# Rate and gate columns of the last two layers: weights stationary in four column groups, summed by a small product

## What is computed

```python
proj = h @ w_in                      # (256 tokens) x (1024) @ (1024) x (3592)
aq, ak, av, dn_qkv, dn_z, dn_b, dn_a = jnp.split(proj, cuts, axis=-1)
...
qkv = jax.nn.silu(causal_dwconv(dn_qkv, dn_conv_w)).astype(jnp.float32)
dq, dk, dv = jnp.split(qkv, [DELTA_K_WIDTH, 2 * DELTA_K_WIDTH], axis=-1)
beta = jax.nn.sigmoid(dn_b.astype(jnp.float32))
g = -jnp.exp(dn_a_log.astype(jnp.float32)) * jax.nn.softplus(
    dn_a.astype(jnp.float32) + dn_dt_bias.astype(jnp.float32))
```

## Time and profile before

| | |
|---|---|
| median of three runs | 1790.45 us (1787.21 to 1792.16) |
| profiled execution, span | 1787.4 us; the page gives no time around the span, so this stands for the execution's own time |
| TensorE busy (matmul) | 1560.1 us, 87% |
| VectorE, ScalarE, GpSimd busy | 53%, 30%, 33% |
| L926, both layers | 64 records, 8.1 us |
| L936, both layers | 48 records, 8.6 us |
| L942, both layers | 64 records, 27.9 us |

### The profile page before, as it was taken

One profiled execution on the slowest core, in us unless ns is written; L12 is line 12 of the kernel. 1 busy time (PEld: TensorE's weight loads), 2 busy tenths in 40 slices (PEclk: granted clock), 3 DMA queues, 4 the chain that ended last, 5 costly groups with the idle time before them and its releaser, 6 DMA issues.

```text
span 1787.4 us, 18463 instructions
## 1 busy us (share of the span) xinstructions
PE 1560.1 (87%) x5998; PEld 953.2 (53%) x5998; DVE 953.6 (53%) x2199; ACT 538.4 (30%) x1472; POOL 584.2 (33%) x595
## 2 busy tenths in 40 slices
PE   8998888986877676556469999999999999999997
PEld 2645463443444222222125867777774778677774
DVE  2586677767686868788873464212123335321222
ACT  2234334442433343323222363211111354211111
POOL 0000046777777777777750012100000002100000
PEclk9999999998989898777789999999999999999999
DMA  9965059999999999999996220844441421364410
GB/s 349 350 224 196 19 219 408 409 409 388 409 398 409 409 409 409 379 408 406 406 404 236 94 95 1 276 159 142 142 176 37 176 95 48 117 230 160 141 48 24
DMA packets 170581, 438.50 MB, mean 245 GB/s; under 512 B 12515, under 2 KB 58883, under 8 KB 170356
## 3 DMA queue, kind: packets, MB, share of 16 engines
q0 software_dynamic: 81824, 299.86, 43.0%
q1 hardware_dynamic: 88662, 137.46, 22.1%
HBM read 436.23 MB, written 1.05 MB: 245 GB/s over the span
## 4 chain that ended last, share of the span: by engine, by line
PE 56%; DMA 14%; DVE 10%; POOL 9%; issue 6%; DVEq 2%; ACT 2%; ACTq 0%; SPq 0%; POOLq 0%
PE psum L1150 15%; DMA arena<-in_expert_u,indices 14%; PE psum L1161 6%; POOL arena L1293 5%; PE psum L914 5%; POOL arena L1288 4%; DVE arena L2196 3%; PE psum L855 2%; PE psum L1175 2%; PE psum L452 2%; PE psum L1138 2%; PE psum L831 2%; PE psum L942 2%; PE psum L538 2%; PE psum L1104 1%
## 5 line engine op out<-in xcount | busy, mean ns | idle before, releaser
L817 PE MATMUL psum<-arena 128*128 128x512 f32 x382 | 240.8, 716 | 193.1 <-ACT arena L1561 189.9
L2196 DVE CUSTOM_DVE_ANT_0 arena<-arena,psum 128x1024 f32<-128x1024 f32 x224 | 273.6, 1221 | 125.6 <-DMA arena<-in_expert_u,indices 107.4
L1293 POOL DMA_INDIRECT arena<-in_expert_v,indices x256 | 255.5, 998 | 79.8 <-issue 70.7
L1288 POOL DMA_INDIRECT arena<-in_expert_u,indices x256 | 251.5, 983 | 89.5 <-issue 61.9
L1150 PE MATMUL psum<-activations_T,weight_ring 128*128 128x256 f32 x1280 | 279.2, 379 | 0.0
L1150 PEld LDWEIGHTS psum<-activations_T,weight_ring 128*128 128x128 f32 x1280 | 243.0, 190 | 39.8 <-issue 7.7
L817 PEld LDWEIGHTS psum<-arena 128*128 128x128 f32 x382 | 69.7, 213 | 335.5 <-ACT arena L1561 307.1
L2437 DVE SCALAR_TENSOR_TENSOR arena<-psum,small,arena 128x254 f32<-128x254 f32 (+1 forms) x176 | 76.8, 477 | 321.2 <-ACT arena L1714 317.9
L818 PE MATMUL psum<-arena 128*128 128x512 f32 x382 | 223.2, 670 | 0.0
L1243 POOL TENSOR_TENSOR small<-small 128x1 f32<-128x1 f32 (+4 forms) x29 | 30.4, 1049 | 539.7 <-DVE small L2309 199.2
L1549 ACT ACTIVATE activations_T<-activations_T 128x1 f32<-128x1 f32 x256 | 51.9, 203 | 396.8 <-DVE activations_T L2196 396.7
(11 more groups left out here) (402 smaller groups left out, 2056.1 us busy)
## 6 DMA issues: line engine op xcount, KB each, us to landing
weight_ring<-in_ffn_w_in SPq DMA_DIRECT2D x44, 1024.0 KB, 7.7
weight_ring<-in_w_in SPq DMA_DIRECT2D x14, 2048.0 KB, 10.3
arena<-in_ffn_w_out POOLq DMA_DIRECT2D x22, 1024.0 KB, 5.2
weight_ring<-in_w_ada SPq DMA_DIRECT2D x8, 2048.0 KB, 8.6
weight_ring<-in_w_out SPq DMA_DIRECT2D x6, 2048.0 KB, 7.8
weight_ring<-in_w_ada SPq DMA_DIRECT2D x16, 512.0 KB, 9.9
weight_ring<-in_w_pq SPq DMA_DIRECT2D x4, 2048.0 KB, 15.7
weight_ring<-in_w_in SPq DMA_DIRECT2D x2, 2080.0 KB, 8.0
```

The costliest lines, as they stand in the source:

```text
L817: mm(o0, DIAG[:, j % ND, :], VROWS[n % NV][:, 0:512], start=m == 0, stop=last)
L1288: nc.gpsimd.indirect_dma_start(UROWS[g % NU], None, a["expert_u"], bass.IndirectOffsetOnAxis(ap=where, axis=0)).then_inc(sem(f"u_row{g % N ...
L1293: nc.gpsimd.indirect_dma_start(VROWS[g % NV], None, a["expert_v"], bass.IndirectOffsetOnAxis(ap=where, axis=0)).then_inc(sem(f"v_row{g % N ...
L2196: ttr(out=DOTJ[n >= UNIT], in0=UROWS[n % NU], in1=h2, scale=1.0, scalar=0.0, op0=ALU.mult, op1=ALU.add, accum_out=DOT[:, i, m:m + 1]).then ...
```

## The change

The eight columns are computed the other way round: the weights are stationary and the 256 tokens move. 32 weight columns (488 to 519 of the slot, the last eight of them the wanted ones) are loaded into one of four column groups of the array, group k modulo 4 for the k-th block of 128 rows of the contraction. Each group adds up two of the eight blocks, on its own 32 partitions of one bank: eight products instead of sixteen. ScalarE copies the bank, 128 partitions by 256, to `BAC`. TensorE then takes two small products, one for each tile of 128 tokens, with `BAC` stationary and a 128x8 matrix `FOUR` moving. `FOUR` picks the wanted eight rows of each group, so the product adds the four groups and turns the result to tokens by eight columns. These small products stand between `wh` 0 and `wh` 1 of the transposes, and wait for the copy. ScalarE's two small copies move along with them. `FOUR` is made once, early, by three small additions on VectorE.

```diff
+        BAC = v(C0 + 12800, SEQ)
...
+        FOUR = small(8)
...
                 w = weights(520)
                 o = bank_a()
-                for i in range(2):
-                    for k in range(KT):
-                        ins = mm(o[:, i * 8:i * 8 + 8], XTP[:, k, i * P:(i + 1) * P], w[:, k, 512:520], start=k == 0, stop=k == KT - 1)
+                for k in range(KT):
+                    g = 32 * (k % 4)
+                    ins = mm(o[g:g + 32, 0:SEQ], w[:, k, 488:520], XTP[:, k, :], start=k < 4, stop=k >= 4)
                 ins.then_inc(a_full, 1)
-                m["ba"] = c["a"]
+                summed_cols = c["a"]
 
                 m["tq"] = []
                 for wh in range(3):
+                    if wh == 1:
+                        pe.wait_ge(a_free, summed_cols)
+                        pe.wait_ge(sem("four_ready"), 1)
+                        o = bank_a()
+                        for i in range(2):
+                            ins = mm(o[:, i * 8:i * 8 + 8], BAC[:, i * P:(i + 1) * P], FOUR, start=True, stop=True)
+                        ins.then_inc(a_full, 1)
+                        m["ba"] = c["a"]
                     pe.wait_ge(sem("cv_silu"), 6 * L + 2 * wh + 2)
...
                 o = full()
-                ob = o[:, 0:16].rearrange("p (i n) -> p i n", i=2)
-                act.copy(BT[:, :, :], ob[:, :, 0:4])
-                act.copy(ST1[:, :, :], ob[:, :, 4:8]).then_inc(a_free, 1)
+                act.copy(BAC, o[:, 0:SEQ]).then_inc(a_free, 1)
                 for wh in range(3):
+                    if wh == 1:
+                        o = full()
+                        ob = o[:, 0:16].rearrange("p (i n) -> p i n", i=2)
+                        act.copy(BT[:, :, :], ob[:, :, 0:4])
+                        act.copy(ST1[:, :, :], ob[:, :, 4:8]).then_inc(a_free, 1)
...
+            tt(FOUR, ident[:, 24:32], ident[:, 56:64], ALU.add)
+            dve.drain()
+            tt(FOUR, FOUR, ident[:, 88:96], ALU.add)
+            dve.drain()
+            tt(FOUR, FOUR, ident[:, 120:128], ALU.add).then_inc(sem("four_ready"), 1)
             all_of(weighted(4))
```

More of the change, by code:

```diff
@@ L281, in program @@
         MON = v(C0 + 6144, 2, D)
-        assert C0 + 12800 <= AR_N
+        BAC = v(C0 + 12800, SEQ)
         SS, MS, RS, HALF, MX, SM, RC, MN = (small(32) for _ in range(8))
```

## The result

The changed kernel takes 1792.15 us in the median of 15 runs (1790.53 to 1796.24), the kernel before 1790.58 in 15 runs beside it (1785.59 to 1793.72). The ratio is 1.0018, with a 95% interval of 1.001 to 1.0027: slower by some 3 us, small but clear of the noise. It isn't the quotient of the two medians, which differ by 1.6 us; the means of the 15 runs differ by 2.9. Two later comparisons gave 1.0011 (0.9989 to 1.0034) and 1.0021 (1.0008 to 1.0034). One of the ten runs of the changed kernel in the first of these took 5314 us; as a slow run it has no part in the ratio.

What follows compares the result with a forecast made beforehand. ScalarE's Silus were taken to bound layer 0's stretch, TensorE at the low clock layer 1's. With the clock high, +0.81 and -1.43 give -0.62 us: 1790.45 to 1789.8 us, range 1785.5 to 1795.6.

Steps and rivals of the forecast that it cites:

- What bounds: From L914's end to L942's start: ScalarE sets the end at the high clock (layer 0), TensorE at the low (layer 1).
- First products: Grouped products replacing L926: 16 records in the time of nine, 1.94 us, off the chain; ends 1.8 and 6.5 us.
- Copy, small products, order: Behind the sixth Silu: copy 0.37 us, small products 0.45, 16 transposes 1.75 instead of 12; +0.81 us a high-clock layer.
- Why the clock should stay: Layer 1's clock fell during eight-column products; these go and 256 columns stream, so it stays high: -1.43 us there.
- The rival of the clock in both layers: Clock falls over small products and transposes, 2.0 us more a layer; in both layers +3.4, 1793.8 us; chance 0.13.
- The base: Profiled stretch from L914's end to L942's start in the kernel before: 7.21 us in layer 0, 9.45 in layer 1.
- Low clock into dn_z for 3.4 us a layer: Rival: 6.8 us low stretch from the small products into L942 in each layer; together +6.2, 1796.6 us; chance 0.07.
- What was hidden: `FOUR` at about 42 us, VectorE's wait moved 1.4 us later, and the next loads were to cost nothing.

Runs made afterwards that it cites:

- one group: Changed kernel with all eight first products in one column group of 32, small products contracting over 32: 1788.88 us, ratio to the kernel before 0.9982.
- the filler: Changed kernel plus eight overwritten products of 128 stationary and 256 moving columns a layer, ahead of the grouped ones: 1789.07 us, ratio to before 0.999.
- the widened kernel: Kernel before with 128 weight columns moving instead of 8 in each of the 16 products a layer: 1787.97 us, ratio 0.9984; repeated, 0.9981.
- the kernel before with the products left out: Kernel before with one product for each tile instead of eight in the rate and gate columns: 1788.62 us, ratio 0.9989.

## Why the prediction was wrong

The forecast was 0.62 us less, no change that can be told; measured was a ratio of 1.0018. The direction was wrong. The time of 1792.15 us lies inside the stated range of 1785.5 to 1795.6 all the same, because the range had been drawn to take in the rival that came true; that is no merit of the forecast. The measurement also told 0.18% from no change, where the prediction had taken 0.3% to be the limit.

*What bounds.* Right: in layer 0 ScalarE's Silus, with L926 off the chain; in layer 1 the clock.

*First products.* The term was off by nearly two: 1.94 us forecast from pairs of row groups, 1.07 measured. Sixteen records that take 3.64 us in one group take 1.07 in four, 3.4 times as fast. By the Trainium skill (TensorEngine Tiling (Array Packing), section Theoretical Speedup) up to four times was to be had; the trace comes near it, with 3.4. Off the chain, the size seemed not to matter. But it set how long TensorE waited: 2.39 us, not 1.3. Whether the clock would have held behind a wait of 1.3 us no run shows; with 3.64 us of products (one group) it did.

*Copy, small products, order.* Forecast +0.81 us a layer, measured +0.92 with the clock held by the filler: copy 0.26 instead of 0.37, small products 0.61 instead of 0.45, 16 transposes 1.80 instead of 1.75.

*The clock.* This is the step that failed: "Why the clock should stay". It looked at what the change puts into the place of the eight-column products, and not at what stood there for the rest of the time: waits of 2.39 us and then of 0.55 to 1.24. The stretch was to be 8.02 us in both layers, +0.81 and -1.43; it was 10.24 and 10.23, +3.03 and +0.78, with the clock at 0.50. The rival of the clock in both layers had the mechanism and the size: 2.0 us a layer forecast, 10.24 - 8.13 = 2.11 measured. It had a chance of 0.13. By the Trainium skill (TensorE: Matmul & The Clock Gate, section Part 4) transposes don't count as work, which pointed to it. As a rule the traces don't bear this out: 24 transposes with a wait of 0.5 us stood at 1.00 in the widened kernel, and in the kernel before with the products left out the clock rose to 1.00 when TensorE had run nothing but transposes for 3.2 us. What part they have in the fall stays open, since no run took transposes apart from waits.

*The base.* Layer 0 of the one profile (7.21 us) was read as the state of the kernel before. A second profile had 7.98 and 7.90; the mean of four is 8.14. Against it the change costs 2 x 2.1 = 4.2 us, and 0.2 to 0.95 more in the dn_z products of a layer: 4.9 to 6.1 in all by the three profiles, as an estimate. The first comparison gave 3.2 (1.8 to 4.8), the two later ones 2.1 and 3.8. That the times show less than the profiles is left open: four layers are a thin base for the kernel before, and no run shows what else gives time back.

*Low clock into dn_z for 3.4 us a layer.* In part right: with 2.1 us in the stretch and 0.2 to 0.95 in dn_z the low clock costs 2.3 to 3.1 us a layer, near this rival's 3.4. The low stretch has the length that it took, about 6.8 us, but begins 0.5 to 2 us ahead of the small products.

*What was hidden.* Right: VectorE's later wait, `FOUR`, and the loads don't appear in the chains of the changed kernel from the groups' end to the turn of the queries.

## What to carry to other kernels

Before work is taken off TensorE beside another engine's chain, ask what it will do there instead, and what is queued behind the wait: at the low clock it takes about twice as long. Give it real work from later on (here half a dn_z tile, 0.9968), or make a narrow product wider where a record costs the same (0.9984). And read a stretch that depends on the clock in more than one profile before it is taken as the base.

## What the runs showed that was not expected

Weights of 32 columns in four column groups run beside each other almost fully, in float32 with two records a product: 1.07 us for 16 records of 256 columns, 3.64 in one group. No wait at the change of shape is visible: the eight transposes behind the single group start at once (1035.59 us, where the products end at 1035.66). And 32 unbroken records of eight columns can leave TensorE at 1.2 GHz, while 32 of 128 columns in the same 3.7 us kept 2.4 GHz in all four layers that were looked at. Transposes alone stood in front of a rise back to 2.4 GHz in two layers.
